# Applying the input's 1/rms after the products, in a two-block transformer kernel on one core

## The chip, the cores and the metric

The kernel runs on one core of one Trainium2 chip. The metric is the device time of one execution in microseconds (us). Before the change, three runs gave 1636.93, 1638.70 and 1638.99 us, so the median is 1638.7 us.

## What is computed

The reference runs two transformer blocks over the same 512 tokens of width 1024, one after the other, in fp32. Only the first stage of the first block matters here:

```
h = x * rsqrt(mean(x*x) + EPS) * g_mix
z = h @ w_in
c_q, c_kv, k_r, hq, hf_f, hf_b, hi, hg = split(z, IN_SPLITS)
a = mla(c_q, c_kv, k_r, ...)
r = hgrn2(hq, hf_f, hf_b, hi, hg, ...)
x = x + concat(a, r) @ w_o
```

`mla` normalises c_q, c_kv and every head's q and k again and attends; `hgrn2` is a gated linear attention over the other five parts of z.

## The kernel before, in words

Activations lie feature-major: a tile is 128 features by 512 tokens, and `h_hi`, `h_lo` hold eight of them (k = 0 to 7). Every fp32 value is kept as a rounded high part and a rest, so a product is three matmuls (`three`, lines 379 to 381). Weights come in slabs of 128x2048 values through a ring of three buffers. SyncE loads slab g when TensorE is done with slab g-3, ScalarE rounds it (`split`, line 1826, into `slab_hi`) and VectorE subtracts (`split`, line 1057, into `slab_lo`). `split(g)` in the text is that pair of steps for slab g. Each engine has a program written out by hand in a fixed order; nothing is scheduled. A wait is on a semaphore's count. `take(name, bank)` is TensorE's wait until the last tile in that PSUM bank has been read.

The head of the kernel: SyncE loads constants, the four 128x1024 blocks of x (`x_tm`), then the slabs. ScalarE and GpSimd issue 23 small loads of gain vectors as rows (`row_program`). TensorE turns x, 32 transposes of 128x128 (line 504), turns the gain rows (line 510), and then turns x a second time as a matmul with a diagonal of 1/rms (line 516), so that the banks hold the normalised h. ScalarE squares the blocks of x (line 1860), takes roots, does split(0), and writes `h_hi` times `g_mix` (line 1868); VectorE copies the turned x to the residual (line 1104), makes the diagonals, does its half of split(0), and writes `h_lo` (line 1130). Slab 0 then starts (`slab_fm(0, ...)`).

Slabs 0 and 1 give c (four tiles), slab 2 k_r, slabs 3 and 4 the tiles z0, z1, z4, z5, slab 5 q, slab 6 k and v, slab 7 z8, z9, slab 8 half of `hi`. From MIX (slab 9) on, a loop over n = 0 to 7 mixes one slab's products with attention units and one direction of one linear-attention head. Its z tiles are 2, 3 (n = 0), 6, 7 (n = 1), 10, 11 (n = 2), `hi` (n = 3), 16, 17 (n = 4), 18, 19 (n = 5); slabs of w_o follow (n = 6, 7). Those tiles use banks 0 and 1 in turn. In the loop ScalarE empties them (`plain`: tile t = 1 of a slab in the next iteration, right behind ScalarE's split; tile t = 0 in the same iteration) and applies Silu or Sigmoid later (`in_place`). Tiles 0, 1, 4, 5, 8, 9 ScalarE activates straight out of PSUM (`activated`, line 1894).

VectorE's iteration n is, in order: the row maximum for the softmax, the mask, the weights, `prepare(n + 1)` (a scan and two subtractions), split(MIX + n + 1), the second half with the states of the linear attention. ScalarE's iteration is: transposed weights, logs, exponentials, split(MIX + n + 1), in-place activations, gate keys and decays, transposed weights.

Of the kernel before, what the change touches and what calls it, by code (L numbers as in the profile page):

```python
# [110 lines left out]
def program(nc, x, p, positions, g_mix, w_in, g_qa, g_kva, w_qb, w_kvb, g_qn, g_kn, lb_param, g_hgo, w_o,  # L111
# [236 lines left out]
    def tensor_program():  # L348
# [170 lines left out]

        def piece(g, t, part):  # L520
# [22 lines left out]
            else:  # L543
# [3 lines left out]
                if part == 1:  # L547
                    ps = tile[name].ps
                elif g < MIX:
                    ps = take(name, b, z_act, z_direct[name[1]])  # L550
                else:
                    ps = take(name, b)
# [1888 lines left out]
```

## Time and profile before

| | us |
|---|---|
| median of three runs | 1638.7 |
| the profiled execution | 1637.87 |
| its span, first to last instruction | 1636.6 |
| TensorE busy | 1610.0 (98%) |
| VectorE busy | 875.6 (54%) |
| ScalarE busy | 655.8 (40%) |
| granted TensorE clock, mean | 0.997 |

Busy time says how long an engine had an instruction in it. A timeline row gives the start, the length, the engine, the line of the kernel, the operation, what it writes and reads, and in brackets the engine's idle time just ahead of it with what ended it. An "x6" row is six instructions back to back, so its length less one instruction's own, over five, is their pace. In the rows PE is TensorE, DVE VectorE, ACT ScalarE.

### The profile page before, as it was taken

How to read it: one execution, taken by the hardware profiler on the slowest of the kernel's cores; microseconds unless marked ns; L12 is line 12 of the kernel's file. 1: busy time of each engine (PE TensorE's matmuls, PEld its weight loads, DVE VectorE, ACT ScalarE, POOL GpSimd, SP SyncE). 2: the span in 40 equal slices, each digit the busy share in tenths (PEclk: the TensorE clock that was granted, in tenths of full speed). 3: DMA queues.
4: the chain of work that ended last, by engine and by line, in shares of the span. 5: the costliest groups of instructions: out<-in, count | busy, mean ns of one | idle time of the engine just before them, and what ended most of it. 6: DMA issues, size and time to landing. Idle time of an engine off the chain costs nothing.

```text
span 1636.6 us, 18068 instructions
## 1 busy us (share of the span) xinstructions
PE 1610.0 (98%) x7569; PEld 1320.1 (81%) x7569; DVE 875.6 (54%) x1164; ACT 655.8 (40%) x789; POOL 11.7 (1%) x25
## 2 busy tenths in 40 slices
PE   7999999999999999999999999999998999999998
PEld 6776777888888888888798888888886878888887
DVE  6447556674444441257655644354445787766313
ACT  4546658543232221155443433223334444444212
POOL 1000000000000000000000000000000000000000
PEclk9999999999999999999999999999999999999999
DMA  5211110123333223223231133222323232332232
GB/s 166 91 59 58 46 52 26 65 65 111 108 103 103 90 91 103 102 98 103 86 103 52 54 107 103 81 88 90 103 77 104 77 103 82 99 103 92 102 103 77
DMA packets 117200, 144.25 MB, mean 88 GB/s; under 512 B 6009, under 2 KB 103632, under 8 KB 117120
## 3 DMA queue, kind: packets, MB, share of 16 engines
q1 hardware_dynamic: 115696, 139.87, 26.1%
q0 software_dynamic: 1232, 3.16, 0.6%
q8 instruction: 60, 0.98, 0.2%
q14 instruction: 20, 0.16, 0.0%
q10 hardware_dynamic: 192, 0.07, 0.0%
HBM read 140.99 MB, written 2.10 MB: 87 GB/s over the span
## 4 chain that ended last, share of the span: by engine, by line
PE 93%; DVE 3%; ACT 2%; issue 1%; DMA 0%; SPq 0%; DVEq 0%; ACTq 0%
PE bank L379 28%; PE bank L381 27%; PE bank L380 27%; PE bank L902 1%; DVE slab_lo L1057 1%; PE bank L665 1%; PE bank L683 1%; PE bank L664 1%; ACT slab_hi L1826 1%; PE bank L728 1%; PE bank L885 1%; PE bank L440 1%; DVE tmp L1771 1%; PE bank L609 1%; PE bank L723 0%
## 5 line engine op out<-in xcount | busy, mean ns | idle before, releaser
L379 PE MATMUL bank<-h_hi,slab_hi 128*128 128x512 f32 x1192 | 471.2, 395 | 5.0 <-DVE h_lo L1062 3.1
L1057 DVE TENSOR_TENSOR slab_lo<-slab_raw,slab_hi 128x2048 fp32r<-128x2048 f32 x130 | 296.1, 2278 | 327.6 <-ACT slab_hi L1826 327.3
L381 PE MATMUL bank<-h_hi,slab_lo 128*128 128x512 f32 x1192 | 464.8, 390 | 0.0
L380 PE MATMUL bank<-h_lo,slab_hi 128*128 128x512 f32 x1192 | 464.5, 390 | 0.0
L1826 ACT ACTIVATE slab_hi<-slab_raw 128x2048 fp32r<-128x2048 f32 x130 | 246.4, 1897 | 173.3 <-DMA slab_raw<-in_w_down 142.9
L379 PEld LDWEIGHTS bank<-h_hi,slab_hi 128*128 128x128 f32 x1192 | 224.2, 188 | 56.9 <-issue 9.1
L380 PEld LDWEIGHTS bank<-h_lo,slab_hi 128*128 128x128 f32 x1192 | 224.3, 188 | 47.1 <-issue 1.4
L381 PEld LDWEIGHTS bank<-h_hi,slab_lo 128*128 128x128 f32 x1192 | 224.0, 188 | 47.2
L1099 DVE TENSOR_TENSOR tmp<-bank,x_rstd_rows 128x512 f32<-128x512 f32 x98 | 66.5, 687 | 94.8 <-PE bank L381 94.7
L379 PE MATMUL bank<-slab_hi,h_hi 128*128 128x256 f32 (+1 forms) x224 | 74.8, 334 | 0.0
L381 PE MATMUL bank<-slab_hi,h_lo 128*128 128x256 f32 (+1 forms) x224 | 73.6, 329 | 0.0
L380 PE MATMUL bank<-slab_lo,h_hi 128*128 128x256 f32 (+1 forms) x224 | 73.5, 328 | 0.0
L379 PE MATMUL bank<-slab_hi,hid_hi 128*128 128x512 f32 x176 | 68.6, 389 | 0.8 <-issue 0.8
L379 PE MATMUL bank<-hid_hi,slab_hi 128*128 128x512 f32 x176 | 68.5, 389 | 0.8 <-issue 0.8
L381 PE MATMUL bank<-hid_hi,slab_lo 128*128 128x512 f32 x176 | 68.5, 389 | 0.0
L380 PE MATMUL bank<-hid_lo,slab_hi 128*128 128x512 f32 x176 | 68.5, 389 | 0.0
L380 PE MATMUL bank<-slab_lo,hid_hi 128*128 128x512 f32 x176 | 68.5, 389 | 0.0
L381 PE MATMUL bank<-slab_hi,hid_lo 128*128 128x512 f32 x176 | 68.5, 389 | 0.0
L2326 ACT ACTIVATE tmp<-tmp,param_cols 128x512 f32<-128x512 f32 x44 | 35.1, 814 | 76.8 <-DVE tmp L1099 76.8
L379 PE MATMUL bank<-y_hi,slab_hi 128*128 128x512 f32 x128 | 50.3, 393 | 0.0
L381 PE MATMUL bank<-y_hi,slab_lo 128*128 128x512 f32 x128 | 49.8, 389 | 0.0
L380 PE MATMUL bank<-y_lo,slab_hi 128*128 128x512 f32 x128 | 49.8, 389 | 0.0
(407 smaller groups left out, 2142.1 us busy)
## 6 DMA issues: line engine op xcount, KB each, us to landing
slab_raw<-in_w_in SPq DMA_DIRECT2D x40, 1024.0 KB, 5.0
slab_raw<-in_w_up SPq DMA_DIRECT2D x33, 1024.0 KB, 5.0
slab_raw<-in_w_down SPq DMA_DIRECT2D x22, 1024.0 KB, 4.9
slab_raw<-in_w_gate SPq DMA_DIRECT2D x11, 1024.0 KB, 5.1
slab_raw<-in_w_o SPq DMA_DIRECT2D x4, 1024.0 KB, 4.9
slab_raw<-in_w_ple_gate SPq DMA_DIRECT2D x4, 1024.0 KB, 5.1
slab_raw<-in_w_ret_o SPq DMA_DIRECT2D x4, 1024.0 KB, 5.2
slab_raw<-in_w_sgu_o SPq DMA_DIRECT2D x4, 1024.0 KB, 4.9
```

Of the source, the lines that this page charges most:

```text
L379: T.matmul(ps, a_hi, b_hi, start=start, stop=False, skip_group_check=skip)
L380: T.matmul(ps, a_hi, b_lo, start=False, stop=False, skip_group_check=skip)
L381: return T.matmul(ps, a_lo, b_hi, start=False, stop=stop, skip_group_check=skip)
L440: ins = T.matmul(dst[:, t:t + 1], sq[:, chunk[t]], ones[:, 0:1], start=clear and t == 0, stop=last, skip_group_check=True)
L609: ins = T.matmul(sums[:, c:c + which.shape[1]], tmp[n % 4][:, chunk[t]], which, start=n == 0 and t == 0, stop=n >= 5, skip_group_check=True)
L664: T.matmul(ps[:, :], q_nope[:, hd, chunk[j]], k_nope[:, hd, :], start=True, stop=False)
L665: whole(("score", u), T.matmul(ps[:, :], q_rope[half, hd // 2, chunk[j]], k_rope[half, hd // 2, :], start=False, stop=True))
L683: ins = T.matmul(ps[:, :], v_mla[:, kb, hd * VH:(hd + 1) * VH], p_t[:, kb, :], start=kb == 0, stop=kb == TT - 1)
L1057: V.tensor_tensor(w_lo[j][:, 0:n], raw[j][:, 0:n], w_hi[j][:, 0:n].bitcast(F32), ALU.subtract).then_inc(slab_lo, 1)
L1099: V.tensor_tensor(dst, t.ps[:, :], xrow[:, :], ALU.mult).then_inc(t.free, 1)
L1826: A.activation(w_hi[j][:, 0:n], raw[j][:, 0:n], ACT.Copy).then_inc(slab_hi, 1)
L2326: A.activation(acc[t], hid[t], ACT.Identity, scale=col("conv_w1", f[t]), bias=col("conv_b_2", f[t])).then_inc(conv_mid, 1)
```

## The change

x is turned once. `h_hi` and `h_lo` are made from x times g_mix without 1/rms, and 1/rms is multiplied into the products on their way out of PSUM: feature-major tiles by VectorE with a 128x512 tile `xrow` that holds the 512 factors in every partition (`feature`, `scaled`, line 1099), the two `hi` tiles by ScalarE with a factor per partition (`scaled_tm`). `xrow` comes from one matmul of ones with the diagonals, behind slab 1. c is left without the factor; its own normalisation takes eps divided by it squared (`xeps`). ScalarE no longer empties z tiles; all its Silu and Sigmoid of z are in place, behind VectorE's product.

In the order of work: SyncE loads slab 0 between the second and the third block of x. All 23 gain rows are issued by ScalarE's queue. TensorE turns the blocks one by one, with the gain rows behind the second. VectorE copies the first two turned tiles between the first `h_lo` tiles and the other six behind split(1).

```diff
         T.wait_ge(consts_landed, 16)
-        for k in range(KT):
-            ps = take(("x", k), (4, 5, 6, 7, 0, 1, 2, 3)[k])
-            for t in range(TT):
-                if k == 0:
-                    T.wait_ge(x_landed[t], 16)
-                ins = T.transpose(ps[:, chunk[t]], x_tm[:, t, k * P:(k + 1) * P], ident)
-            whole(("x", k), ins)
-        T.wait_ge(rows_landed, 16 * n_rows[0])
-        T.wait_ge(rows_landed_act, 16 * n_rows[1])
-        ps = take("cols", rot())
-        for blk in range(3):
-            ins = T.transpose(ps[:, chunk[blk]], rows[:, blk, :], ident)
-        whole("cols", ins)
-        for k in range(KT):
-            ps = take(("h", k), rot(), h_lo_done, k + 1)
-            for t in range(TT):
-                T.wait_ge(x_diag_done, t + 1)
-                ins = T.matmul(ps[:, chunk[t]], x_tm[:, t, k * P:(k + 1) * P], x_diag[:, t, :], start=t == 0, stop=True,
-                               skip_group_check=True)
-            whole(("h", k), ins)
+        xs = [take(("x", k), k) for k in range(KT - 1)]
+        for t in range(TT):
+            T.wait_ge(x_landed[t], 16)
+            for k in range(KT - 1):
+                ins = T.transpose(xs[k][:, chunk[t]], x_tm[:, t, k * P:(k + 1) * P], ident)
+                if t == TT - 1:
+                    whole(("x", k), ins)
+            if t == 1:
+                T.wait_ge(rows_landed, 16 * n_rows)
+                ps = take("cols", KT - 1)
+                for blk in range(3):
+                    ins = T.transpose(ps[:, chunk[blk]], rows[:, blk, :], ident)
+                whole("cols", ins)
+        ps = take(("x", KT - 1), KT - 1)
+        for t in range(TT):
+            ins = T.transpose(ps[:, chunk[t]], x_tm[:, t, (KT - 1) * P:KT * P], ident)
+        whole(("x", KT - 1), ins)
...
         slab_fm(0, [("c", 0), ("c", 1)], ready=h_ready(0))
         slab_fm(1, [("c", 2), ("c", 3)])
+        T.wait_ge(x_diag_done, 1)
+        ps = take("x_row", rot())
+        whole("x_row", T.matmul(ps[:, :], ones, x_diag[:, :, :].rearrange("p t c -> p (t c)"), start=True, stop=True))
         T.wait_ge(slab_lo, 3)
...
         V.wait_ge(consts_landed, 16)
-        def input_diagonal(t):
-            V.wait_ge(x_std, t + 1)
-            V.wait_ge(vector_step, step(V.reciprocal(xcol[:, t:t + 1], xcol[:, t:t + 1])))
-            V.tensor_scalar(x_diag[:, t, :], ident, xcol[:, t:t + 1], None, ALU.mult).then_inc(x_diag_done, 1)
-        for k in range(KT):
-            copied(("x", k), xT[:, k, :])
-            if k in (1, 3, 5):
-                input_diagonal(k // 2)
         t = tile["cols"]
         V.wait_ge(psum_ready, t.done)
         V.tensor_copy(cols[:, :], t.ps[:, 0:3 * P]).then_inc(t.free, 1)
         emptied("cols")
-        input_diagonal(TT - 1)
         split(0)
         for k in range(KT):
             V.wait_ge(h_hi_done, k + 1)
-            V.scalar_tensor_tensor(h_lo[:, k, :], tile["h", k].ps[:, :], col("g_mix", k), h_hi[:, k, :].bitcast(F32),
+            V.scalar_tensor_tensor(h_lo[:, k, :], tile["x", k].ps[:, :], col("g_mix", k), h_hi[:, k, :].bitcast(F32),
                                    ALU.mult, ALU.subtract).then_inc(h_lo_done, 1)
+            if k < 2:
+                copied(("x", k), xT[:, k, :])
+        split(1)
+        for k in range(2, KT):
+            copied(("x", k), xT[:, k, :])
+        V.wait_ge(x_std, TT)
+        V.wait_ge(vector_step, step(V.scalar_tensor_tensor(xeps[:, :], xcol[:, :], EPS, xcol[:, :], ALU.mult, ALU.mult)))
+        V.wait_ge(vector_step, step(V.reciprocal(xcol[:, :], xcol[:, :])))
+        diagonal(x_diag[:, :, :].rearrange("p t c -> p (t c)"), xcol[:, :], x_diag_done)
         L0, L1 = (cols[:, ROWS["lb_param"] + 8 * k:ROWS["lb_param"] + 8 * (k + 1)] for k in range(2))
...
+        split(2)
...
+        V.wait_ge(psum_ready, t.done)
+        V.tensor_copy(xrow[:, :], t.ps[:, :]).then_inc(t.free, 1)
+        V.wait_ge(t.free, t.value)
+        scaled("kr", kr_raw[:, 0, :])
         V.wait_ge(sines_done, 1)
         V.tensor_scalar(sin1, turns, sign_col, None, ALU.mult).then_inc(rope_tables, 1)
         V.wait_ge(rope_tables, 1)
-        rstd(rcol[:, 0:2 * TT], "csum")
+        t = tile["csum"]
+        V.wait_ge(psum_ready, t.done)
+        V.scalar_tensor_tensor(rcol[:, 0:2 * TT].rearrange("p (j t) -> p j t", j=2),
+                               t.ps[:, 0:2 * TT].rearrange("p (j t) -> p j t", j=2), 1.0 / LORA,
+                               xeps[:, :].unsqueeze(1).broadcast_to([P, 2, TT]), ALU.mult, ALU.add).then_inc(t.free, 1)
+        V.wait_ge(lora_std, 1)
+        V.wait_ge(vector_step, step(V.reciprocal(rcol[:, 0:2 * TT], rcol[:, 0:2 * TT])))
         for j in range(2):
             diagonal(tmp[2 * j + 1], rcol[:, TT * j:TT * (j + 1)], lora_diag)
         split(4)
@@ -1187,6 +1190,9 @@
             V.wait_ge(c_hi_done, n + 1)
             V.tensor_tensor(c_lo[n], tmp[4 + n], c_hi[n].bitcast(F32), ALU.subtract).then_inc(c_lo_done, 1)
...
+        def feature(f):
+            scaled(("z", f), zt[:, f, :])
...
         V.wait_ge(masks_landed, 16)
         rotated(0, kr_raw[:, 0, :])
+        feature(0)
+        feature(1)
         split(6)
+        feature(4)
+        feature(5)
         for t in range(6):
             copied(("q", t), q_nope[:, t, :] if t < HEADS else q_rope[:, t - HEADS, :])
         for n in range(2):
...
         rotated(1, q_rope[:, 0, :])
         rotated(2, q_rope[:, 1, :])
+        feature(8)
+        feature(9)
         V.wait_ge(vector_step, gains)
...
+        def out_of_psum(s):
+            g, t = MIX + s // 2, s % 2
+            if g < WO and g != HI2:
+                feature(z_tiles[g] + t)
...
             if n >= 6:
...
             weights(unit)
+            out_of_psum(2 * n)
...
+        def input_squares(t):
             A.wait_ge(x_landed[t], 16)
-            A.wait_ge(scalar_step, step(A.activation(x_sq[:, t, :], x_tm[:, t, :], ACT.Square,
-                                                     accum_out=xcol[:, t:t + 1])))
-            A.activation(xcol[:, t:t + 1], xcol[:, t:t + 1], ACT.Sqrt, bias=eps_col, scale=1.0 / D).then_inc(x_std, 1)
+            squares_step[t] = step(A.activation(x_sq[:, t, :], x_tm[:, t, :], ACT.Square, accum_out=xcol[:, t:t + 1]))
+        input_squares(0)
+        input_squares(1)
         split(0)
+        input_squares(2)
         emptied("cols")
         for k in range(KT):
-            t = tile["h", k]
+            t = tile["x", k]
             A.wait_ge(psum_ready, t.done)
             A.activation(h_hi[:, k, :], t.ps[:, :], ACT.Identity, scale=col("g_mix", k)).then_inc(h_hi_done, 1)
+        split(1)
+        input_squares(3)
+        for t in range(TT):
+            A.wait_ge(scalar_step, squares_step[t])
+            A.activation(xcol[:, t:t + 1], xcol[:, t:t + 1], ACT.Sqrt, bias=eps_col, scale=1.0 / D).then_inc(x_std, 1)
+        split(2)
         for n in range(2):
...
-        def activated(f, fn):
-            t = tile["z", f]
-            A.wait_ge(psum_ready, t.done)
-            A.activation(zt[:, f, :], t.ps[:, :], fn).then_inc(z_act, 1)
+        def in_place(f, fn):
+            emptied(("z", f))
+            A.activation(zt[:, f, :], zt[:, f, :], fn).then_inc(z_act, 1)
         def values(n, t):
-            ps = tile["hi", n, t]
-            A.wait_ge(psum_ready, ps.done)
-            A.activation(v_hg[:, 2 * t:2 * t + 2, n * CW:(n + 1) * CW], ps.ps[:, :].rearrange("p (u c) -> p u c", u=2),
-                         ACT.Copy).then_inc(ps.free, 1)
+            scaled_tm(("hi", n, t), v_hg[:, 2 * t:2 * t + 2, n * CW:(n + 1) * CW], 2 * t, ACT.Identity)
...
             A.wait_ge(psum_ready, tile["crow", j].done)
         squares(0, kr_raw[:, 0, :])
         split(5)
-        activated(4, ACT.Sigmoid)
-        activated(5, ACT.Sigmoid)
         split(6)
+        in_place(0, ACT.Silu)
+        in_place(1, ACT.Silu)
+        in_place(4, ACT.Sigmoid)
+        in_place(5, ACT.Sigmoid)
         for t in range(6):
             emptied(("q", t))
             squares(1 + t, q_nope[:, t, :] if t < HEADS else q_rope[:, t - HEADS, :])
...
-        def plain(s):
-            g, t = MIX + s // 2, s % 2
-            if g == HI2:
-                values(1, t)
-            elif g < WO:
-                copied(("z", z_tiles[g] + t), zt[:, z_tiles[g] + t, :])
...
             keys(n)
             split(MIX + n + 1)
-            if n:
-                plain(2 * n - 1)
+            if n == 4:
+                values(1, 1)
...
+            if n == 3:
+                values(1, 0)
             if n in VALUES_ODD:
                 attn_out(VALUES_ODD[n])
...
         A.wait_ge(rows_zeroed, 1)
+        n = 0
         for r, src in loads:
             for at in ((0, ROPE) if src.shape[1] == ROPE else (0,)):
-                k = int(n_rows[0] > n_rows[1])
                 dst = rows[r % P:r % P + src.shape[0], r // P, at:at + src.shape[1]]
-                (G, A)[k].dma_start(dst, src).then_inc((rows_landed, rows_landed_act)[k], 16)
-                n_rows[k] += 1
+                A.dma_start(dst, src).then_inc(rows_landed, 16)
...
+        for t in range(2):
             SP.dma_start(x_tm[:, t, :], x[0, t * P:(t + 1) * P, :]).then_inc(x_landed[t], 16)
         for g, (columns, srcs) in enumerate(slabs):
+            if g == 1:
+                for t in range(2, TT):
+                    SP.dma_start(x_tm[:, t, :], x[0, t * P:(t + 1) * P, :]).then_inc(x_landed[t], 16)
             if g >= RING:
                 SP.wait_ge(psum_ready, slab_end[g - RING])
             k = srcs[0].shape[1]
```

Three places of the order. First, VectorE's queue at the start: before, up to the eight `h_lo` tiles,

```order
L1104 COPY residual<-bank 128x512 x2
L1124 COPY param_cols<-bank 128x384
L1115 RECIPROCAL x_rstd_cols<-x_rstd_cols 128x1
L1116 TENSOR_SCALAR x_diagonals<-const_small_sb,x_rstd_cols 128x128
L1057 TENSOR_TENSOR slab_lo_58<-slab_raw_55,slab_hi_61 128x2048
L1130 SCALAR_TENSOR_TENSOR h_lo<-bank,param_cols,h_hi 128x512 x8
```

and now:

```order
L1108 COPY param_cols<-bank 128x384
L1051 TENSOR_TENSOR slab_lo_59<-slab_raw_56,slab_hi_62 128x2048
L1113 SCALAR_TENSOR_TENSOR h_lo<-bank,param_cols,h_hi 128x512
L1098 COPY residual<-bank 128x512
L1113 SCALAR_TENSOR_TENSOR h_lo<-bank,param_cols,h_hi 128x512
L1098 COPY residual<-bank 128x512
L1113 SCALAR_TENSOR_TENSOR h_lo<-bank,param_cols,h_hi 128x512 x6
```

The copies moved from ahead of split(0) to between and behind the `h_lo` tiles. Second, VectorE's queue where q comes out of PSUM (`slab_lo_58` or `_59` there is split(6)): before,

```order
L1194 TENSOR_TENSOR tmp_71<-bank,rope_sin 128x512
L1196 TENSOR_TENSOR kr_raw<-kr_raw,rope_cos 128x512
L1197 TENSOR_TENSOR kr_raw<-kr_raw,tmp_71 128x512
L1057 TENSOR_TENSOR slab_lo_58<-slab_raw_55,slab_hi_61 128x2048
L1104 COPY q_nope<-bank 128x512 x4
```

and now:

```order
L1203 TENSOR_TENSOR kr_raw<-kr_raw,tmp_72 128x512
L1093 TENSOR_TENSOR z<-bank,x_rstd_rows 128x512 x2
L1051 TENSOR_TENSOR slab_lo_59<-slab_raw_56,slab_hi_62 128x2048
L1093 TENSOR_TENSOR z<-bank,x_rstd_rows 128x512 x2
L1098 COPY q_nope<-bank 128x512 x4
```

Four products of z stand ahead of the first q copy. Third, VectorE's queue in iteration n = 6, with the last z tile (19): before,

```order
L1278 TENSOR_TENSOR tmp_70<-z 128x512
L1279 TENSOR_TENSOR tmp_71<-z 128x512
L1104 COPY z<-bank 128x512
L1057 TENSOR_TENSOR slab_lo_59<-slab_raw_56,slab_hi_62 128x2048
L1318 COPY gla_states<-bank 128x128
```

and now:

```order
L1290 TENSOR_TENSOR tmp_71<-z 128x512
L1291 TENSOR_TENSOR tmp_72<-z 128x512
L1098 COPY z<-bank 128x512
L1051 TENSOR_TENSOR slab_lo_60<-slab_raw_57,slab_hi_63 128x2048
L1093 TENSOR_TENSOR z<-bank,x_rstd_rows 128x512
L1330 COPY gla_states<-bank 128x128
```

Bank 1 with tile 19 was emptied by ScalarE (line 1840) behind its own half of split(16), and is now emptied by VectorE behind VectorE's half.

## Rows read from the trace of the kernel before

**Rows 1.** The page, part 4: the chain that ended last, shares by engine.

```profile
PE 93%; DVE 3%; ACT 2%; issue 1%; DMA 0%; SPq 0%; DVEq 0%; ACTq 0%
```

**Rows 2.** Timeline of TensorE, 0 to 26 us: start, length, engine, line, operation, idle before.

```profile
9.99 6.34 PE L504 MATMUL bank<-const_small_sb,x_tm 128*128 128x128 f32 x29 [1.21 <-DMA x_tm<-in_x]
...
24.66 0.48 PE L379 MATMUL bank<-h_hi,slab_hi 128*128 128x512 f32 x1
```

**Rows 3.** Timeline of ScalarE and its DMA queue, 0 to 26 us.

```profile
1.30 0.54 ACTq L2373 DMA_DIRECT2D param_rows<-in_g_qa  x1
...
5.28 0.34 ACTq L2373 DMA_DIRECT2D param_rows<-in_g_kn  x1
...
7.05 1.04 ACT L1860 ACTIVATE x_squares<-x_tm 128x1024 f32<-128x1024 f32 x1
...
12.60 1.91 ACT L1826 ACTIVATE slab_hi<-slab_raw 128x2048 fp32r<-128x2048 f32 x1
```

**Rows 4.** Timeline of all engines, 77.7 to 85 us.

```profile
80.98 2.28 DVE L1057 TENSOR_TENSOR slab_lo<-slab_raw,slab_hi 128x2048 fp32r<-128x2048 f32 x1
...
83.18 1.88 DVE L1104 COPY q_nope<-bank 128x512 f32<-128x512 f32 x3
...
84.58 0.61 PE L609 MATMUL bank<-const_small_sb,tmp 128*128 128x1 f32 x4 [0.70 <-ACT tmp L1914]
```

**Rows 5.** Timeline of all engines, 121 to 126 us.

```profile
124.04 0.74 DVE L1234 SCALAR_TENSOR_TENSOR k_nope<-k_nope,query_key_gain,bank 128x512 f32<-128x512 f32 x1
...
125.51 0.67 PE L655 MATMUL bank<-tmp,const_small_sb 128*128 128x512 f32 x1 [0.74 <-DVE k_rope L1235]
```

**Rows 6.** One tensor's instructions, param_rows, 0 to 30 us: issue to landing.

```profile
DMA to landing us min/median/max: 4.8/5.0/5.1
```

**Rows 7.** Timeline of TensorE, 1262 to 1266 us.

```profile
1262.43 0.76 PE L379 MATMUL bank<-h_hi,slab_hi 128*128 128x512 f32 x1 [3.14 <-DVE h_lo L1062]
...
1265.48 0.40 PE L380 MATMUL bank<-h_lo,slab_hi 128*128 128x512 f32 x1
```

**Rows 8.** Busy time by stretch: us, then PE, PEld, DVE, ACT, POOL, granted clock, DMA.

```profile
1262.00:1263.00 1.00, 0.57 (x2) 0.50 (x3) 1.00 (x3) 0.10 (x2) 0.00 (x0) 0.50 0.00 0
```

**Rows 9.** Timeline of TensorE, 51 to 53 us.

```profile
51.52 0.39 PE L380 MATMUL bank<-h_lo,slab_hi 128*128 128x512 f32 x1
51.75 0.39 PE L381 MATMUL bank<-h_hi,slab_lo 128*128 128x512 f32 x1
52.27 0.50 PE L379 MATMUL bank<-h_hi,slab_hi 128*128 128x512 f32 x1
```

**Rows 10.** The chain that ended last, 56 to 80 us: start, length, what.

```profile
65.30 1.72 PE bank L585 x4
```

**Rows 11.** Timelines of all engines, 172 to 189 us.

```profile
172.36 2.28 DVE L1057 TENSOR_TENSOR slab_lo<-slab_raw,slab_hi 128x2048 fp32r<-128x2048 f32 x1
...
173.35 1.15 ACT L2024 ACTIVATE z<-z 128x512 f32<-128x512 f32 x2
...
179.83 0.78 ACT L1946 ACTIVATE tmp<-bank,softmax_cols,query_scale 128x512 f32<-128x512 f32 x1 [0.53 <-DVE softmax_cols L1246]
...
185.10 0.69 DVE L1245 TENSOR_REDUCE softmax_cols<-bank 128x1 f32<-128x512 f32 x1 [0.59 <-PE bank L665]
...
187.97 0.66 PE L674 MATMUL bank<-const_small_sb,tmp 128*128 128x128 f32 x4
```

**Rows 12.** Timeline of all engines, 276 to 284 us.

```profile
277.02 2.28 DVE L1057 TENSOR_TENSOR slab_lo<-slab_raw,slab_hi 128x2048 fp32r<-128x2048 f32 x1
...
277.36 1.15 ACT L2024 ACTIVATE z<-z 128x512 f32<-128x512 f32 x2
...
283.40 1.12 PE L683 MATMUL bank<-weights_t,v_mla 128*128 128x512 f32 x2 [0.96 <-ACT weights_t L1956]
```

**Rows 13.** Timeline of all engines, 296 to 299.5 us.

```profile
296.62 0.50 PE L379 MATMUL bank<-attn_hi,slab_hi 128*128 128x512 f32 x1 [0.24 <-ACT z L1840]
...
296.92 2.28 DVE L1057 TENSOR_TENSOR slab_lo<-slab_raw,slab_hi 128x2048 fp32r<-128x2048 f32 x1
```

More of the change, by code:

```diff
@@ L137, in program @@
     xcol = sb("x_rstd_cols", [P, TT])
+    xeps = sb("x_scaled_eps", [P, TT])
     lbc = sb("lower_bounds", [P, 4, 8])
@@ L191, in program @@
     c_lo = [cq_lo[:, 0, :], cq_lo[:, 1, :], ckv_lo[:, 0, :], ckv_lo[:, 1, :]]
-    kr_raw = slot("kr_raw", 24, 1)
-    reset = xrow[:, :]
+    kr_raw, reset = slot("kr_raw", 16, 1), slot("scan_reset", 24, 1)[:, 0, :]
     q_nope, q_rope = slot("q_nope", 25, 4), slot("q_rope", 29, 2)
@@ L546, in piece @@
                 b = t if g >= MIX else 2 * (g % 2) + t
[L547 to L552, printed above, removed]
+                ps = tile[name].ps if part else take(name, b)
                 for k in range(4 * part, 4 * part + 4):
@@ L1140, in vector_program @@
         gains = steps[0]
+        copied(("c", 0), c_raw[:, 0, :])
+        copied(("c", 1), c_raw[:, 1, :])
+        split(2)
         V.wait_ge(positions_landed, 16)
@@ L1171, in vector_program @@
         split(3)
-        copied("kr", kr_raw[:, 0, :])
+        t = tile["x_row"]
+        V.wait_ge(psum_ready, t.done)
+        V.tensor_copy(xrow[:, :], t.ps[:, :]).then_inc(t.free, 1)
+        V.wait_ge(t.free, t.value)
+        scaled("kr", kr_raw[:, 0, :])
         V.wait_ge(sines_done, 1)
@@ L1369, in vector_program @@
             split(MIX + n + 1)
+            if n:
+                out_of_psum(2 * n - 1)
             if n >= 6:
@@ L1857, in scalar_program @@
         A.activation(rcol[:, 0:1], eps_col, ACT.Sqrt)
-        for t in range(TT):
+        squares_step = {}
+        def input_squares(t):
             A.wait_ge(x_landed[t], 16)
-            A.wait_ge(scalar_step, step(A.activation(x_sq[:, t, :], x_tm[:, t, :], ACT.Square,
-                                                     accum_out=xcol[:, t:t + 1])))
-            A.activation(xcol[:, t:t + 1], xcol[:, t:t + 1], ACT.Sqrt, bias=eps_col, scale=1.0 / D).then_inc(x_std, 1)
+            squares_step[t] = step(A.activation(x_sq[:, t, :], x_tm[:, t, :], ACT.Square, accum_out=xcol[:, t:t + 1]))
+        input_squares(0)
+        input_squares(1)
         split(0)
+        input_squares(2)
         emptied("cols")
         for k in range(KT):
-            t = tile["h", k]
+            t = tile["x", k]
             A.wait_ge(psum_ready, t.done)
             A.activation(h_hi[:, k, :], t.ps[:, :], ACT.Identity, scale=col("g_mix", k)).then_inc(h_hi_done, 1)
+        split(1)
[4 more added lines that the diff above has]
+        split(2)
         for n in range(2):
@@ L1888, in scalar_program @@
         A.activation(turns, angle, ACT.Sin).then_inc(sines_done, 1)
-        def activated(f, fn):
-            t = tile["z", f]
-            A.wait_ge(psum_ready, t.done)
-            A.activation(zt[:, f, :], t.ps[:, :], fn).then_inc(z_act, 1)
+        def in_place(f, fn):
+            emptied(("z", f))
+            A.activation(zt[:, f, :], zt[:, f, :], fn).then_inc(z_act, 1)
         def values(n, t):
-            ps = tile["hi", n, t]
-            A.wait_ge(psum_ready, ps.done)
-            A.activation(v_hg[:, 2 * t:2 * t + 2, n * CW:(n + 1) * CW], ps.ps[:, :].rearrange("p (u c) -> p u c", u=2),
-                         ACT.Copy).then_inc(ps.free, 1)
+            scaled_tm(("hi", n, t), v_hg[:, 2 * t:2 * t + 2, n * CW:(n + 1) * CW], 2 * t, ACT.Identity)
         split(4)
-        root("csum", rcol[:, 0:2 * TT], tile["csum"].ps[:, 0:2 * TT], LORA)
-        activated(0, ACT.Silu)
-        activated(1, ACT.Silu)
+        emptied("csum")
+        A.activation(rcol[:, 0:2 * TT], rcol[:, 0:2 * TT], ACT.Sqrt).then_inc(lora_std, 1)
         for n in range(4):
@@ L1934, in scalar_program @@
         split(8)
-        activated(8, ACT.Sigmoid)
-        activated(9, ACT.Sigmoid)
+        in_place(8, ACT.Sigmoid)
+        in_place(9, ACT.Sigmoid)
         def weights_exp(u):
@@ L2012, in head_output @@
             A.activation(g_hi[:, hd, :], zt[:, 4 + hd, :], ACT.Copy).then_inc(gla_hi, 1)
-        def plain(s):
-            g, t = MIX + s // 2, s % 2
-            if g == HI2:
-                values(1, t)
-            elif g < WO:
-                copied(("z", z_tiles[g] + t), zt[:, z_tiles[g] + t, :])
-        def in_place(f, fn):
-            emptied(("z", f))
-            A.activation(zt[:, f, :], zt[:, f, :], fn).then_inc(z_act, 1)
         A.wait_ge(bounds_done, 1)
```

17 lines of the change are left out of this document (4 added, 13 removed).

## The prediction

> **What bounds the kernel now.** I read the page first. Its chain gives TensorE 93% of the span [rows 1], so an edit is worth what it adds to or takes from TensorE's queue, or the time for which it keeps TensorE waiting. Then I read the head (0 to 25 us) engine by engine, and after it the two hundred microseconds in which the products of slabs 3 to 14 are emptied, looking for every place where TensorE already stands against VectorE or ScalarE. There are few, each under 1 us; the part on VectorE's products takes them one by one. A wait that is already there has no slack, so work put ahead of its cause is paid in full.
>
> **The head.** Slab 0 starts at 24.66 us [rows 2]. Where will it start?
> - ScalarE issues 11 gain loads from 1.30 to 5.28 + 0.34 = 5.62 us [rows 3], 0.39 us each. With 23 it ends at 1.30 + 23 x 0.39 = 10.3. From its last issue to the first square took 7.05 - 5.62 = 1.43 us [rows 3], so squares start at 11.7. Two squares at 1.04 each [rows 3] and a read-out, taken as 1.15, end at 14.0; split(0) takes 1.9 [rows 3] and ends at 15.9. Slab 0 itself has long landed.
> - VectorE's half starts there. In the trace one such subtraction holds VectorE for 83.18 - 80.98 = 2.2 us [rows 4]: 18.1. Then come h_lo 0, a copy, h_lo 1, a copy. A read of a bank with two operands has a pace of about 0.66 (my estimate, from 0.74 for one [rows 5] less the overlap that copies show), a copy one of 0.60, since three took 1.88 [rows 4]. With the handover that is 20.9 us. The two copies count, because slab 0's products go to banks 0 and 1, which hold x's tiles 0 and 1.
> - TensorE must have turned x by then. Here 29 transposes took 6.34 us [rows 2], 0.21 each. Behind the gain rows lie 3 + 14 + 4 transposes, and tile 0 is whole after about 11 of them, 2.3 us. The gain loads that the trace shows took 4.8 to 5.1 us from issue to landing [rows 6], so the last lands at about 15 and tile 0 is whole by 17.3: in time.
>
> So slab 0 starts 24.66 - 20.9 = 3.8 us earlier. Bounds: 2.2 (two squares or issues dearer) to 4.7.
>
> **The clock.** TensorE will be idle from about 19 to 21 and before that from 8 until the rows land. After a stretch with short matmuls and 3.14 us idle, the trace shows it restarting at a granted clock of 0.50, the lower of the two levels, 1.2 GHz [rows 7, 8]. Seven matmuls start in the 3.05 us from 1262.43 to 1265.48; at the full pace of 0.23 us (two matmuls lie between 51.75 less 0.46 and 51.98 [rows 9]) they take 1.6. The loss is 1.4 us, and I take that. Bounds: 0 (no drop), and 3.0, if the low level lasts the 6 us of the first transposes [rows 2], whose 0.21 us I read as that level, the page's column notwithstanding.
>
> The Trainium skill, page "TensorE: Matmul & The Clock Gate", section "What's actually happening", says that the default state is throttled and that activity releases the throttle. By it slab 0 starts at 1.2 GHz for certain; without it, the sum below would be 1.4 lower. The granted clock after the idle stretch in rows 7 and 8 agrees with it.
>
> **Removed and added on TensorE.** The second turning (32 diagonal matmuls) goes; its gain is inside the 3.8. The matmul for xrow is new: two 128x512 fp32 products took 1.72 us [rows 10], so 0.86. Between slabs 2 and 3 TensorE waited 52.27 - (51.75 + 0.23) = 0.3 for split(3) [rows 9], which the new matmul now covers. Cost 0.6; bounds 0.5 to 0.9.
>
> **Sixteen products on VectorE.** Each replaces a ScalarE instruction of the same size, and by itself has the price of a copy, 0.60. What counts is where they stand.
> - *q* [rows 4]. Features 0 and 1 stand ahead of split(6), 4 and 5 behind it, all ahead of the first copy of q. VectorE cannot do them earlier: it waits for TensorE's swap tile first. The first q copy, at 83.18, is 4 x 0.60 = 2.4 later, so is ScalarE's square, and TensorE, which waits for that square already, stands 2.4 longer. Bounds 2.0 to 2.8. ScalarE's four in-place activations and its table loads fit before it.
> - *Keys* [rows 5]. Features 8 and 9 stand ahead of the product at 124.04; TensorE's fourth spread waits for the head scaled next: 1.2. Bounds 1.0 to 1.4.
> - *n = 1* [rows 11]. Feature 3 stands behind VectorE's split, which began at 172.36, and ends at about 175.3. ScalarE's second in-place activation began about 173.9 and now waits: 1.4 late, less 0.53 idle, so the exponential is 0.9 late. Feature 6 adds 0.6, which makes 1.5 at the states, less 0.59 idle: the next maximum is 0.9 late, and the transposes at 187.97 follow it with no margin. Cost 0.9; bounds 0 to 1.5.
> - *n = 5* [rows 12]. Feature 17 starts at 277.02 + 2.2 = 279.2 and ends at 279.9. The second of ScalarE's two activations began about 277.9. ScalarE's queue from there to the transposed weights is full, and TensorE waits for them. Cost 2.0; bounds 1.0 to 2.1.
> - *n = 6* [rows 13]. TensorE takes bank 1 at 296.4 and got it at 296.62. Now feature 19 has to free it, and it stands behind the subtraction that starts at 296.92: 299.1 + 0.7 = 299.8. Cost 3.2; bounds 2.5 to 3.3.
> - The other six of the sixteen fall where VectorE idles for longer than they take, and the next maximum waits for TensorE: nothing. If that cover were gone, 0.6 each.
>
> **The sum.** -3.8 + 1.4 + 0.6 + 2.4 + 1.2 + 0.9 + 2.0 + 3.2 = +7.9 us. From 296 us on nothing has changed. The profiled execution took 1637.87, so it would be 1645.8; the median of the runs is 0.8 above that execution, so I say **1646.6**. All terms at their low ends give +2.3, at their high ends +13.
>
> **The rivals.**
> 1. *The head's gain is kept (faster).* The five waits are read off the old schedule. If VectorE reached those products before TensorE's events, all of them would lie in its idle time, as its 54% busy share suggests. Then -3.8 + 0.6 and full clock: 1638.7 - 3.2 = 1635.5, and 1634.6 with the head at its better end. It decides at the swap tile: only if the waits come to less than the head gives back. Against it: VectorE's order is fixed, and three of its five places are behind a split that cannot move.
> 2. *About the same.* Two of the three waits in the loop are absorbed by ScalarE, which loses nine copies; without the 2.0 and the 3.2 the sum is +2.7: 1641.4. For it: those copies stood on ScalarE's own queue. Against it: those at n = 5 and 6 hang on VectorE [rows 12, 13].
> 3. *The low clock lasts (slower still).* 6 us at the lower level at slab 0, and again a restart after the 3.2 us at n = 6: 1.6 + 1.4 more, 1649.6. For it: the restart in [rows 7]. Against it: TensorE is busy right before and after 299.
> 4. *The rows land late (slower still).* 23 loads on one queue beside 4 KB packets of x. Beyond 17 us each microsecond moves slab 0 by one; at 20 us, +3, 1649.6. For it: 5 us for a load [rows 6]. Against it: slab 0's packets are smaller.
>
> **How the numbers follow.** Forecast 0.63, rival 1 0.08, rival 2 0.12, rivals 3 and 4 0.17. A measurement tells about 0.2%, 3.3 us, from no change. Rival 1 and the low edge of rival 2 give faster 0.07; rival 2 mostly and the low ends of the sum give same 0.13; the rest is slower, 0.80. The range reaches from the middle of rival 2's time to beyond rivals 3 and 4: 1640.5 to 1651.5, leaving out rival 1 and the far ends.
>
> **What would show it.** In the profile after: slab 0's first matmul at about 20.9 us and at a granted clock of 0.50; the square's wait at about 3.1 us instead of 0.70; the fourth key spread's at about 1.9; the weights' at n = 5 about 3.0; and for bank 1 at n = 6 a wait of about 3.4 us whose releaser is a VectorE tensor-tensor instead of ScalarE. If TensorE's waits between 60 and 330 us come to no more than the 2.6 us of before (0.70 + 0.74 + 0.96 + 0.24), the forecast is wrong, whatever the head does. If slab 0 starts after 23 us, ScalarE's issues or the rows' landing are dearer than I priced them.

## The result, and the profile after

The changed kernel takes 1653.44 us (median of four runs, 1652.93 to 1654.12) against 1638.85 us (four runs, 1636.93 to 1640.14). The ratio is 1.0092, with a 95% interval of 1.0079 to 1.0104: slower by 14.6 us, and above the 1651.5 us at which the range ended. The profiled execution took 1653.93 us, 16.1 more than the profiled one of before.

The chain on the page answers to [rows 1]: TensorE's share fell by two points, VectorE's rose by two.

```profile
span 1652.6 us, 17944 instructions
PE 91%; DVE 5%; ACT 2%; issue 1%; ACTq 0%; DMA 0%; DVEq 0%
```

The waits of TensorE in the first 330 us, by line (line, what it waited for, us in total, times, longest). The first two rows of the view, TensorE's waits for the gain rows and for x in the head, are left out. Before, the four behind the head came to 2.6 us.

```profile
...
PE bank L378 <- DVE z L1093: 4.0, 2, 3.5
PE bank L603 <- ACT tmp L1937: 3.1, 1, 3.1
PE bank L677 <- ACT weights_t L1981: 2.5, 1, 2.5
PE bank L649 <- DVE k_rope L1247: 2.2, 1, 2.2
PE bank L378 <- DVE residual L1098: 1.9, 1, 1.9
PE bank L668 <- DVE tmp L1266: 0.6, 1, 0.6
```

The ones that are not the head's come to 4.0 + 3.1 + 2.5 + 2.2 + 0.6 = 12.4 us, so 9.8 were added. The forecast had 2.4 + 1.2 + 0.9 + 2.0 + 3.2 = 9.7. The waits, then, were priced well. The rest has to be found elsewhere, and it is best found by following the same TensorE instruction through both traces:

| TensorE instruction | before | after | lag | step | forecast of the step |
|---|---|---|---|---|---|
| slab 0, first matmul | 24.66 | 20.41 | -4.25 | -4.25 | -3.8 |
| slab 0, 25th matmul | 30.21 | 28.70 | -1.51 | +2.7, clock | +1.4 |
| slab 3, third matmul | 52.84 | 51.82 | -1.02 | +0.5, the xrow matmul | +0.6 |
| first sum of the first q square | 84.58 | 85.92 | +1.34 | +2.4 | +2.4 |
| first matmul on c_kv | 92.32 | 98.45 | +6.13 | **+4.8, clock** | 0 |
| first matmul of v | 104.01 | 109.84 | +5.83 | -0.3 | 0 |
| fourth key spread | 125.51 | 132.52 | +7.01 | +1.2 | +1.2 |
| transposed weights, n = 1 | 187.97 | 195.64 | +7.67 | +0.7 | +0.9 |
| the slab's second tile, n = 5 | 279.41 | 287.64 | +8.23 | +0.6 | 0 |
| attention product, n = 5 | 283.40 | 293.13 | +9.73 | +1.5 | +2.0 |
| bank 1, n = 6 | 296.62 | 309.59 | +12.97 | +3.2 | +3.2 |
| states, n = 6 | 299.56 | 314.11 | +14.55 | **+1.6, clock** | 0 |
| block two, 1300 us | 1300.22 | 1316.27 | +16.05 | +1.5, clock | 0 |

With the two rows of n = 5 taken together (2.1 for 2.0), every step of waits and work holds within 0.5 us. Four steps are the clock's. Here is the largest of them, TensorE's timeline of the changed kernel (start, length, engine, line, operation, in brackets the idle time before and what ended it):

```profile
85.92 1.05 PE L603 MATMUL bank<-const_small_sb,tmp 128*128 128x1 f32 x8 [3.10 <-ACT tmp L1937]
...
87.39 0.39 PE L380 MATMUL bank<-cq_hi,slab_lo 128*128 128x512 f32 x1
87.62 0.54 PE L378 MATMUL bank<-cq_hi,slab_hi 128*128 128x512 f32 x1
...
88.38 0.63 PE L380 MATMUL bank<-cq_hi,slab_lo 128*128 128x512 f32 x1
88.81 1.70 PE L603 MATMUL bank<-const_small_sb,tmp 128*128 128x1 f32 x8
...
98.77 0.39 PE L379 MATMUL bank<-ckv_lo,slab_hi 128*128 128x512 f32 x1
99.00 0.40 PE L380 MATMUL bank<-ckv_hi,slab_lo 128*128 128x512 f32 x1
```

TensorE waits 3.10 us for the square. For 1.7 us after it the old pace still holds (87.39 to 87.62, 0.23 us). Then matmuls come 0.43 us apart, and a group of eight one-column sums takes 1.70 us, against 1.05 at 85.92. Near 98 us the pace is 0.23 again (98.77 to 99.00). Busy time by stretch shows it as the granted clock (columns: us; busy us and instructions of PE, PEld, DVE, ACT, POOL; granted clock; DMA):

```profile
20.00:26.00 6.00, 5.59 (x13) 4.46 (x14) 6.00 (x8) 5.98 (x12) 0.00 (x0) 1.00 0.00 0
...
88.00:97.00 9.00, 9.00 (x31) 7.75 (x30) 1.38 (x2) 1.26 (x2) 0.00 (x0) 0.50 0.01 2
...
309.50:313.00 3.50, 3.41 (x8) 2.74 (x9) 0.04 (x1) 3.37 (x5) 0.00 (x0) 0.51 0.02 5
```

A granted clock of 0.50 means 1.2 GHz of the two levels. TensorE was busy all of the 9 us, so what it lost in clock is lost in time. The row of 20 to 26 us needs care: the column says 1.00, but slab 0's matmuls lie 0.43 us apart, as in the low stretches:

```profile
20.41 0.77 PE L378 MATMUL bank<-h_hi,slab_hi 128*128 128x512 f32 x1 [1.93 <-DVE residual L1098]
20.98 0.63 PE L379 MATMUL bank<-h_lo,slab_hi 128*128 128x512 f32 x1
...
25.67 0.63 PE L378 MATMUL bank<-h_hi,slab_hi 128*128 128x512 f32 x1
...
26.41 0.39 PE L380 MATMUL bank<-h_hi,slab_lo 128*128 128x512 f32 x1
26.64 0.40 PE L378 MATMUL bank<-h_hi,slab_hi 128*128 128x512 f32 x1
```

20.98 to 21.40 is 0.42, 26.41 to 26.64 is 0.23. The record of the clock holds nothing ahead of about 26 us in this trace, and the column fills that in with full speed. The pace of equal matmuls is the safer reading.

The loss of 2.7 us at slab 0 belongs to this execution. The experiments q_early, q_half, loop_early and all_moved below have the same head, and in their traces the 24 steps from slab 0's first matmul to its 25th took 7.14 to 7.19 us, against 8.29 here and 5.55 in the kernel before: slab 0 lost 1.6 us there.

The wait at n = 6 answers to [rows 13]. VectorE first, then TensorE:

```profile
306.66 2.28 DVE L1051 TENSOR_TENSOR slab_lo<-slab_raw,slab_hi 128x2048 fp32r<-128x2048 f32 x1
308.86 0.68 DVE L1093 TENSOR_TENSOR z<-bank,x_rstd_rows 128x512 f32<-128x512 f32 x1
```

```profile
309.59 0.80 PE L378 MATMUL bank<-attn_hi,slab_hi 128*128 128x512 f32 x1 [3.47 <-DVE z L1093]
310.19 0.63 PE L379 MATMUL bank<-attn_lo,slab_hi 128*128 128x512 f32 x1
310.62 0.63 PE L380 MATMUL bank<-attn_hi,slab_lo 128*128 128x512 f32 x1
...
313.32 0.39 PE L378 MATMUL bank<-attn_hi,slab_hi 128*128 128x512 f32 x1
313.56 0.40 PE L379 MATMUL bank<-attn_lo,slab_hi 128*128 128x512 f32 x1
```

Feature 19 stands behind the subtraction as foreseen (308.86), and TensorE waits 3.47 us. The first matmuls behind it are at the lower level at once.

### The profile page after: what moved, and what is told of

Same layout as the page of the kernel before. It is cut to its first block, busy times and chain, and to the rows that moved or that the text cites. A ratio compares the mean times of both kernels' runs of the same rounds, so it can differ in the third digit from the quotient of the medians.

```text
span 1652.6 us, 17944 instructions
## 1 busy us (share of the span) xinstructions
PE 1613.5 (98%) x7507; PEld 1322.3 (80%) x7507; DVE 884.5 (54%) x1177; ACT 650.8 (39%) x783; POOL 5.6 (0%) x13
## 4 chain that ended last, share of the span: by engine, by line
PE 91%; DVE 5%; ACT 2%; issue 1%; ACTq 0%; DMA 0%; DVEq 0%
PE bank L378 27%; PE bank L380 27%; PE bank L379 27%; DVE slab_lo L1051 1%; PE bank L896 1%; PE bank L659 1%; PE bank L722 1%; PE bank L658 1%; PE bank L677 1%; PE bank L879 1%; PE bank L603 1%; PE bank L439 1%; DVE tmp L1792 1%; PE bank L717 0%; ACT slab_hi L1847 0%
```

## The experiments

**Theory.** A wait of TensorE of about 3 us costs itself and then a stretch of several us at the lower clock; shorter ones cost themselves alone. (The second half did not hold everywhere, as all_moved and the part on the prediction show.) **Rivals.** The low clock comes from the work there (groups of one-column matmuls), or from chance; or its cost grows with the wait, however short.

### q_early: the q features where VectorE idles

```diff
-        V.wait_ge(masks_landed, 16)
-        rotated(0, kr_raw[:, 0, :])
         feature(0)
         feature(1)
         split(6)
         feature(4)
         feature(5)
+        V.wait_ge(masks_landed, 16)
+        rotated(0, kr_raw[:, 0, :])
```

> The changed kernel with features 0, 1, 4 and 5 and split(6) put ahead of VectorE's wait for the first swap tile; nothing else moved. Theory (a wait of about 3 us costs itself and then a stretch at the lower clock): TensorE's 3.10 us at the square of q falls to 0.3 or less, and the low clock behind it, worth 4.6 us of lag, goes too: 1653.4 - 3.0 - 4.6 = 1645.8 us. Rival (the low clock comes from the work there or from chance, not from the wait): only the wait goes, 1650.4 us, and the granted clock still falls near 90 us.

Measured: 1644.84 us (five runs, 1643.02 to 1647.45), 8.6 below the changed kernel; 1.0037 of the kernel before (1.0024 to 1.0050). The wait is gone altogether, and so is the low clock:

```profile
84.00:90.00 6.00, 6.00 (x40) 5.38 (x39) 2.47 (x4) 1.78 (x3) 0.00 (x0) 1.00 0.01 3
```

3.1 us of the 8.6 are the wait. The work of this stretch is the same as in the changed kernel, with its one-column sums, and runs at full clock: the rival of the work falls.

### q_half: two of the four

```diff
+        feature(0)
+        feature(1)
         V.wait_ge(masks_landed, 16)
         rotated(0, kr_raw[:, 0, :])
-        feature(0)
-        feature(1)
         split(6)
```

> The changed kernel with only features 0 and 1 ahead of the wait for the swap tile; 4 and 5 stay between it and q. TensorE's wait becomes 3.1 - 1.2 = 1.9 us. The changed kernel's waits of 2.50 and 2.2 us were followed by no low clock. Theory with a cliff: no low clock either, 1653.4 - 1.2 - 4.6 = 1647.6 us. Rival (the clock's cost grows with the wait, 4.6 for 3.1): half of it stays, 1650 us. Rival (nothing to do with the wait): 1652.2 us.

Measured: 1648.84 us (1647.64 to 1650.88), 4.6 below the changed kernel. By time alone this lies as near to a cost that grows with the wait as to the cliff (a cost that is either there in full or not at all). The trace decides:

```profile
84.62 1.05 PE L603 MATMUL bank<-const_small_sb,tmp 128*128 128x1 f32 x8 [1.90 <-ACT tmp L1937]
...
87.02 0.95 PE L603 MATMUL bank<-const_small_sb,tmp 128*128 128x1 f32 x8
```

```profile
85.00:90.00 5.00, 5.00 (x35) 4.49 (x34) 1.31 (x3) 1.40 (x3) 0.00 (x0) 1.00 0.02 3
```

A wait of 1.90 us, and no low clock at all behind it. Of the 4.6 us, 1.2 are shorter wait and the rest is clock, so two products of 0.6 us on VectorE, at this place, cost about four times their length. Why the median is 1.2 us above my sum is not settled; the four runs lie in two pairs, near 1647.7 and near 1650.4, and the low stretches at n = 6 and in block two differ in length from one execution to another.

### before_q_wait: the wait alone, in the kernel before

```diff
+        for i in range(4):
+            V.tensor_tensor(xT[:, 2 + i, :], xT[:, 2 + i, :], xT[:, 2 + i, :], ALU.max)
         for t in range(6):
             copied(("q", t), q_nope[:, t, :] if t < HEADS else q_rope[:, t - HEADS, :])
```

> The kernel before with four extra VectorE instructions of 128x512 (a maximum of a residual tile with itself, 0.6 us each) ahead of the first copy of q. Theory: TensorE's wait grows from 0.70 to 3.1 us and a stretch of low clock follows: 1638.9 + 2.4 + 4.6 = 1645.9 us. Rival (the clock fell for another part of the change): 1641.3 us and a full clock near 90 us.

Measured: 1647.04 us (1645.05 to 1649.60), 1.0052 of the kernel before (1.0037 to 1.0067), 8.4 us more for 2.4 us of VectorE. The kernel before, with nothing of the change in it, now shows the wait and the low clock:

```profile
87.00 1.05 PE L609 MATMUL bank<-const_small_sb,tmp 128*128 128x1 f32 x8 [3.12 <-ACT tmp L1916]
...
89.62 1.70 PE L609 MATMUL bank<-const_small_sb,tmp 128*128 128x1 f32 x8
```

```profile
88.00:102.00 14.00, 14.00 (x49) 12.01 (x49) 3.38 (x6) 3.84 (x5) 0.00 (x0) 0.54 0.06 11
```

This is the clearest of the runs: one wait lengthened from 0.70 to 3.12 us, and 14 us at 0.54 follow. That part of the change's cost has nothing to do with what is computed. The stretch is longer than the changed kernel's: by the lag of the first matmul of v it cost 6.1 us here, against 4.8 at the changed kernel's first matmul on c_kv. That fits a time of 1.1 us above the expectation, though block two lost 1.6 us more as well in this execution.

Chance is ruled out by the other traces. The clock fell at q in all five whose wait there was 3.09 to 3.12 us (the changed kernel, before_q_wait, loop_early, warm_gap2, warm_both), and in none of the other five (1.90 us or less). At n = 6 it fell in all five with a wait of 3.47 or 3.48 us, and in none of the other five (0.24 us or none).

### loop_early: the second tiles of the loop

```diff
             weights_max(unit)
+            if n:
+                out_of_psum(2 * n - 1)
             masked(n)
...
             split(MIX + n + 1)
-            if n:
-                out_of_psum(2 * n - 1)
```

> The changed kernel with the product of each slab's second tile (features 3, 7, 11, 17, 19) ahead of the mask instead of behind the split; q and keys as they are. Theory: the waits of 0.48, 2.50 and 3.47 us fall to those of before (0, 0.96, 0.24), the 0.6 us at n = 1 goes, and so does the low clock after 309 us (1.6): 1653.4 - 5.9 - 1.6 = 1645.9 us. Rival (ScalarE is late at n = 5 for another reason, since its squares and roots stand there): 1.5 of it stays, 1647.4 us.

Measured: 1645.19 us (1643.35 to 1646.28), 8.2 below the changed kernel, 0.7 below the expectation. The waits at n = 1, for the bank at n = 5 and at n = 6 are gone; the transposed weights' fell from 2.50 to 0.5 us, less than before the change. TensorE's bank at n = 6 is now free before it asks, since VectorE does feature 19 while it waits for the mask:

```profile
295.69 0.69 DVE L1093 TENSOR_TENSOR z<-bank,x_rstd_rows 128x512 f32<-128x512 f32 x1
299.03 0.69 DVE L1316 TENSOR_TENSOR gla_scores<-bank,const_mix_sb 128x512 f32<-128x512 f32 x1 [2.66 <-PE bank L686]
```

```profile
296.00:302.00 6.00, 6.00 (x43) 5.53 (x43) 3.31 (x5) 3.22 (x3) 0.00 (x0) 1.00 0.52 175
```

So n = 5 hung on feature 17 alone; the rival (ScalarE late for its own work) falls.

### all_moved: every place mended

q_early and loop_early together, and for the keys:

```diff
         rotated(1, q_rope[:, 0, :])
+        feature(8)
         rotated(2, q_rope[:, 1, :])
-        feature(8)
-        feature(9)
...
             V.tensor_tensor(k_rope[half, hd // 2, :], kr_raw[half, 0, :], ps.ps[half, :], ALU.mult).then_inc(head_done, 1)
+            if hd == 1:
+                feature(9)
```

> The changed kernel with all three moves: the q features early, feature 8 ahead of the last swap and 9 behind the second head, the loop's second tiles ahead of the mask. The head is the change's own. Theory: every wait of TensorE between 60 and 330 us over 0.6 us is gone, and with them the low clock of the first block behind slab 0; what is left is the head's gain 4.2, less slab 0 at the low clock 2.6 and the new matmul 0.6, and less than before of the old waits (0.70 at q, 0.74 at the keys, about 0.5 of the weights, 0.24 at the bank, 2.1 in all): 1638.7 - 1.2 - 2.1 = 1635.4 us. Rival (VectorE, with the products, runs short elsewhere once these places are mended): 1638 us or more, and new waits on VectorE.

Measured: 1635.12 us (eleven runs, 1634.40 to 1636.71), 0.9981 of the kernel before (0.9973 to 0.9990), so 3.0 us faster than it. The sum was 0.3 off, with luck in it: it counts 2.6 us for slab 0 at the low clock, where this trace shows 1.6, and block two lost 1.6 us more to the clock in this execution than in the kernel before. Its waits of TensorE from 60 to 330 us, and the clock at slab 0:

```profile
PE bank L649 <- DVE k_rope L1246: 1.0, 1, 1.0
PE bank L677 <- ACT weights_t L1982: 0.5, 1, 0.5
```

```profile
22.00:25.00 3.00, 3.00 (x8) 2.33 (x8) 3.00 (x5) 3.00 (x8) 0.00 (x0) 0.50 0.00 0
```

Two waits are left, 1.5 us. The one at the keys, 1.0 us, is over the 0.6 us that the theory allowed. In this trace the record of the clock reaches back to slab 0, and shows 0.50 there: what the pace had shown in the changed kernel is the clock's. TensorE's timeline says more of it:

```profile
20.49 0.47 PE L378 MATMUL bank<-h_hi,slab_hi 128*128 128x512 f32 x1 [1.99 <-DVE residual L1098]
...
21.50 0.41 PE L379 MATMUL bank<-h_lo,slab_hi 128*128 128x512 f32 x1
21.72 0.62 PE L380 MATMUL bank<-h_hi,slab_lo 128*128 128x512 f32 x1
22.14 0.63 PE L378 MATMUL bank<-h_hi,slab_hi 128*128 128x512 f32 x1
```

The clock was already up here: 21.50 to 21.72 is 0.22. It fell behind, at 21.72 (0.42 to the next), after a wait of 1.99 us that began 4.7 us behind the end of one of 5.64 us. The traces of q_half and loop_early show the same behind 1.93 us. So the length of one wait does not decide alone; in the middle of full work 1.90, 2.2 and 2.50 us did no harm.

### all_warm, warm_gap2, warm_both: filling TensorE's idle time in the head

In all three, TensorE does the four transposes of x's last tile three times over:

```diff
-        for t in range(TT):
-            ins = T.transpose(ps[:, chunk[t]], x_tm[:, t, (KT - 1) * P:KT * P], ident)
+        for t in range(3 * TT):
+            ins = T.transpose(ps[:, chunk[t % TT]], x_tm[:, t % TT, (KT - 1) * P:KT * P], ident)
```

warm_both also repeats transposes of the second block while TensorE waits for the gain rows:

```diff
             if t == 1:
+                for i in range(26):
+                    T.transpose(xs[i % 7][:, chunk[1]], x_tm[:, 1, (i % 7) * P:(i % 7 + 1) * P], ident)
                 T.wait_ge(rows_landed, 16 * n_rows)
```

> The kernel all_moved, and in TensorE's head the four transposes of x's last tile done three times over, so that the 1.9 us ahead of slab 0 are filled. Theory: TensorE is then busy from 13.7 us to slab 0, the clock rises before or with slab 0 as it did in the kernel before after 6 us of transposes, and up to 2.6 us come back: 1633.0 us. Rival (transposes do not raise the clock, or the 5.6 us wait for the gain rows decides): 1635.5 us, slab 0's first matmuls at 0.43 us each.

> The changed kernel with only that filling of the 1.9 us ahead of slab 0. Theory: slab 0's matmuls come at 0.23 us instead of 0.43 at the latest from the third on, 1653.4 - 2.6 = 1650.8 us. Rival (fills do nothing): 1653.4 us.

> The changed kernel with both gaps filled: 26 repeated transposes of x's second block during the 5.6 us wait for the gain rows too. Theory: TensorE is busy from 4.9 us on and the clock is up before 14 us; slab 0 starts at full clock, 1650.8 us or 0.1 less than warm_gap2. If warm_gap2 is no better than the changed kernel and this one is, the first gap decides. Rival: both at 1653.4 us.

Measured: all_warm 1633.56 us (six runs, 1632.15 to 1633.98), 0.9968 of the kernel before (0.9956 to 0.9979), the fastest of all, 1.6 us below all_moved. warm_gap2 1651.41 us (1650.87 to 1652.72), 2.0 below the changed kernel; as the kernel before, measured beside it, was 0.7 us lower this time (1638.11), the gain against it is 1.3 (13.3 us above it instead of 14.6). warm_both 1653.74 us (1648.92 to 1657.27), no gain.

TensorE's timeline of all_warm, then of warm_both:

```profile
17.43 1.66 PE L513 MATMUL bank<-const_small_sb,x_tm 128*128 128x128 f32 x12
20.42 0.47 PE L378 MATMUL bank<-h_hi,slab_hi 128*128 128x512 f32 x1 [1.32 <-DVE residual L1098]
...
21.42 0.40 PE L379 MATMUL bank<-h_lo,slab_hi 128*128 128x512 f32 x1
21.65 0.39 PE L380 MATMUL bank<-h_hi,slab_lo 128*128 128x512 f32 x1
```

```profile
7.96 4.51 PE L507 MATMUL bank<-const_small_sb,x_tm 128*128 128x128 f32 x26
13.78 0.55 PE L511 MATMUL bank<-const_small_sb,param_rows 128*128 128x128 f32 x3 [1.31 <-DMA param_rows<-in_g_kn]
14.16 1.69 PE L502 MATMUL bank<-const_small_sb,x_tm 128*128 128x128 f32 x14
...
20.09 0.47 PE L378 MATMUL bank<-h_hi,slab_hi 128*128 128x512 f32 x1 [2.93 <-DVE residual L1100]
...
21.37 0.63 PE L380 MATMUL bank<-h_hi,slab_lo 128*128 128x512 f32 x1
21.79 0.63 PE L378 MATMUL bank<-h_hi,slab_hi 128*128 128x512 f32 x1
```

In all_warm the twelve transposes take 1.66 us, most of them at the faster pace, and slab 0 starts with matmuls 0.23 us apart (21.42 to 21.65). The 1.32 us of idle time that are left ahead of slab 0 did no harm. Slab 0's first 24 steps took 5.54 us here and in warm_gap2, the kernel before's pace; that is 1.6 less than in all_moved, and the medians differ by the same 1.6. warm_both is the miss that teaches: its clock rose early (14 transposes took 1.69 us instead of 3.19), so the same twelve fills were through sooner, TensorE then stood still for 2.93 us, and slab 0 fell to 0.43 (21.37 to 21.79). It lost 1.6 us, as much as in all_moved. Being warm early was worth nothing with a wait of 2.93 us in between.

## Why the prediction was wrong

**The head** held: ScalarE's issues ended at 9.6 (10.3 forecast), slab 0 started at 20.41 (20.9), 4.25 us earlier (3.8). The two copies did stand ahead of it, as TensorE's wait on the residual shows.

**Removed and added on TensorE** held: 0.5 for 0.6.

**Sixteen products on VectorE** held in the sum: 2.4 at q (2.4), 1.2 at the keys (1.2), 0.7 at n = 1 (0.9), 3.2 at n = 6 (3.2). At n = 5 the 2.0 came in two parts, 0.6 as TensorE's wait for bank 1, which feature 17 has to free, and 1.5 at the weights. The bank I had not named. The other six products, and ScalarE's in-place activations, cost nothing.

**The clock** is the step that failed. It stood in the sum once, "The loss is 1.4 us, and I take that", for slab 0 alone, and the same mechanism was not asked of the waits that the forecast itself made over 3 us long. It said that TensorE would stand "2.4 longer" behind the 0.70 us at q, thus 3.1, and 3.2 longer at n = 6, thus 3.4, and it put nothing for the clock behind either. q lost 4.8 us by that and n = 6 1.6. Rival 3 had the latter (1.4), not the former, and got too little of the chance. Against it I had put "TensorE is busy right before and after 299". So it was in the kernel after too, and the clock fell all the same.

The 1.4 us for slab 0 was mis-sized as well, by less: 2.7 in the profiled execution, 1.6 in the four other traces with this head. (The pace of 0.23 us that it rests on is right, by the rows at 51.52 and 51.75; the working beside it is not, since three matmuls lie between 51.29 and 51.98.)

[rows 7] were a weaker model than the forecast took them for. They show 3.14 us of idle time and a granted clock of 0.50 behind it, but the clock had fallen ahead of that wait, which began at 1259.29. TensorE and the clock of the kernel before, just ahead of it:

```profile
1255.51 1.05 PE L440 MATMUL bank<-const_small_sb,tmp 128*128 128x1 f32 x8 [1.41 <-DVE tmp L1070]
1257.86 1.43 PE L979 MATMUL bank<-tmp,const_small_sb 128*128 128x512 f32 x2 [1.29 <-DVE tmp L1084]
```

```profile
1258.00:1259.00 1.00, 1.00 (x2) 0.15 (x2) 0.00 (x0) 0.00 (x0) 0.00 (x0) 0.77 0.48 169
```

Two waits of 1.41 and 1.29 us, with 1.05 us of work between them, were enough for the fall here. In the changed kernel it came at the same place, at 1272.1 us, again ahead of its 3.14 us, which began at 1274.45. So it was not this row but the experiments at q and n = 6 that showed what one wait of over 3 us does.

With 2.7 + 4.8 + 1.6 = 9.1 for the clock in place of 1.4, the forecast's own sum of +7.9 becomes +15.6, against 14.6 of the medians and 16.1 of the profiled executions; with 1.6 for slab 0 it becomes +14.5. The 1.5 us of block two are no part of the change: the waits are the same in both kernels, and in this execution the low clock lasted longer, so that the two matmuls ahead of the 3.14 us took 2.08 us instead of 1.43 and eleven matmuls behind it, instead of seven, ran at the lower pace. Stretches of that place were longer or shorter from trace to trace, which may be part of why runs of one kernel differ by 2 us.

The Trainium skill, page "TensorE: Matmul & The Clock Gate", section "What's actually happening", was cited for slab 0, as saying that the default state is throttled and that activity releases the throttle. The changed kernel's trace agrees: slab 0 began at the lower level. "For certain" was too much, though: in the traces of q_half, loop_early and all_moved its first matmuls came 0.23 us apart, the transposes ahead of it having already raised the clock. At q and n = 6 the traces agree with the page too, in that the lower level came with the idle time and the upper came back in busy work (98.77, 313.32); I had applied the rule where the engine starts, and not where it stops.

**The rivals.** Rival 1 lost by the five waits. Rival 2 held that ScalarE would absorb n = 5 and n = 6; it absorbed neither. Rival 3's 6 us at the lower pace at slab 0 came about in the profiled execution (20.41 to 26.10). Rival 4 did not come about: the last gain row landed by 13.7 us. Rival 1's wish, the head's gain without the waits, is what all_moved brings, at 1635.1 us where it said 1635.5, though by an order that the change does not have, and with slab 0 partly at the lower clock, where rival 1 had it at full speed.

## What to carry to other kernels

When an edit makes a wait of the bounding engine longer, price it in two terms: the wait, and the stretch at the lower clock that may follow it. Behind waits of 3.1 to 3.5 us in full work it always followed here, and cost 1.4 to 6.2 us, at q more than the wait itself. Sum the waits of before and the delay added to each, and look at every one that grows past what the trace shows to be harmless, and at short waits that stand close together. An instruction that is given to a half-idle engine costs nothing only where it stands in that engine's idle time: the same sixteen products added 9.8 us of waits in one order and none in another. With the order mended, 14.6 us above the kernel before became 3.0 below it; these 17.6 us are more than the head's start brings (4.2), for whose sake the products stand there.

## What the runs showed of the hardware

- Waits of TensorE in full work, over all ten traces: behind 1.90 (one trace), 2.2 (six) and 2.5 us (five) the clock stayed; with 3.1 (five) and 3.47 us (five) it fell to 0.50. In the head, shortly behind a wait of 5.0 to 5.6 us, it stayed behind 1.23 and 1.32 us and fell with 1.93, 1.99 and 2.60; in warm_both, with 1.31 us before, it fell behind 2.93.
- In block two it fell after waits of only 1.41 and 1.29 us, about 1 us apart: in nine of ten traces ahead of the 3.14 us wait that follows, in all_warm 0.3 us into it. What of the engine's work ahead of a wait decides was not tried.
- The fall did not keep to the end of the wait. The low clock was there with the first matmul behind 3.47 us (0.43 us pace), came 1.7 us late behind 3.10 us (87.62) with the same kind of work, and in warm_gap2 0.3 us ahead of the end of the same wait.
- Low stretches were of different lengths for equal waits: at q 10.2 us in three traces and 13.7 in two, at n = 6 3.4 us in four and 6.8 in one. What sets the length was not tried.
- The clock column of a stretch ahead of the first record of the clock reads 1.00 whatever the pace. Equal matmuls tell the level: 0.23 us for 128x512 at the upper, 0.43 at the lower; transposes of 128x128 0.11 and 0.21.
